# Down products of a two-unit chunk and of the last chunk put in another order, and the last layer's final norms on VectorE alone

## The reference

```python
# first layer (no convolution), hidden width 2816
gate, up = jnp.split(h @ w_ffn_in, 2, axis=-1)
y = (jax.nn.silu(gate) * up) @ w_ffn_out
# second and third layer
def conv_ffn(h, w_up, conv_w, conv_b, w_down):
    u = h @ w_up
    ...                                   # 3-tap convolution along the tokens
    a, g = jnp.split(acc, 2, axis=-1)
    return (jax.nn.silu(g) * a) @ w_down
def layer_norm(x, g, b):
    xf = x.astype(jnp.float32)
    mu = jnp.mean(xf, -1, keepdims=True)
    var = jnp.mean(jnp.square(xf - mu), -1, keepdims=True)
    return ((xf - mu) * lax.rsqrt(var + LN_EPS) * g + b).astype(x.dtype)
x_lat = layer_norm(DN_ALPHA * x_lat + m_lat[5] * f_lat, ln_g[l, 1], ln_b[l, 1])
```

## Time and profile before

| | |
|---|---|
| runs | 2518.44, 2526.46, 2524.96 us; median 2524.96 us |
| profiled execution | 2526.85 us; its span (first to last instruction) 2525.1 us |
| granted TensorE clock, mean | 0.973 of full |
| busy: PE, DVE, ACT, POOL | 2372.2, 1600.2, 974.1, 321.1 us |
| share of the span | 94%, 63%, 39%, 13% |

### The profile page before, as it was taken

One profiled execution on the slowest core, in us unless ns is written; L12 is line 12 of the kernel. 1 busy time (PEld: TensorE's weight loads), 2 busy tenths in 40 slices (PEclk: granted clock), 3 DMA queues, 4 the chain that ended last, 5 costly groups with the idle time before them and its releaser, 6 DMA issues.

```text
span 2525.1 us, 33201 instructions
## 1 busy us (share of the span) xinstructions
PE 2372.2 (94%) x13210; PEld 1915.8 (76%) x13210; DVE 1600.2 (63%) x2718; ACT 974.1 (39%) x1800; POOL 321.1 (13%) x325
## 2 busy tenths in 40 slices
PE   6988998999999899899999999999998999999996
PEld 3866567888888778566778888888887677888875
DVE  3638686565657642677778775556474987765455
ACT  4326453322212522567352232322442774423322
POOL 0210101000012200000100313223111000101223
PEclk9999999999999999999999999999998999999998
DMA  6430015744434212111412342333122103432221
GB/s 253 136 104 1 26 59 175 250 154 150 164 137 157 102 42 77 51 49 43 150 63 84 101 150 77 110 115 133 43 76 76 35 22 130 150 106 95 92 92 50
DMA packets 79162, 257.59 MB, mean 102 GB/s; under 512 B 5664, under 2 KB 10400, under 8 KB 70560
## 3 DMA queue, kind: packets, MB, share of 16 engines
q1 hardware_dynamic: 65024, 205.01, 23.6%
q0 software_dynamic: 12688, 46.14, 5.3%
q10 hardware_dynamic: 1296, 4.30, 0.4%
HBM read 246.00 MB, written 9.44 MB: 101 GB/s over the span
## 4 chain that ended last, share of the span: by engine, by line
PE 70%; DVE 14%; ACT 7%; issue 4%; DMA 2%; POOL 1%; SPq 1%; POOLq 0%; ACTq 0%; DVEq 0%
PE PS L1087 9%; PE PS L1089 9%; PE PS L1088 9%; PE PS L1158 5%; PE PS L1159 5%; PE PS L1160 5%; PE PS L948 4%; PE PS L846 3%; PE PS L843 3%; PE PS L844 3%; PE PS L961 2%; ACT HT L2469 2%; PE PS L992 2%; DVE SM L1833 1%; PE PS L891 1%
## 5 line engine op out<-in xcount | busy, mean ns | idle before, releaser
L1087 PE MATMUL PS<-HH,WH 128*128 128x512 f32 (+1 forms) x1088 | 421.3, 387 | 9.2 <-DVE TMP L2155 4.6
L1088 PE MATMUL PS<-HL,WH 128*128 128x512 f32 (+1 forms) x1088 | 417.7, 384 | 0.0
L1089 PE MATMUL PS<-HH,WL 128*128 128x512 f32 (+1 forms) x1088 | 417.7, 384 | 0.0
L2307 ACT ACTIVATE WH<-STG 128x1024 fp32r<-128x1024 f32 (+1 forms) x204 | 198.9, 1022 | 293.3 <-PE PS L1160 250.3
L2007 DVE TENSOR_TENSOR WL<-STG,WH 128x1024 fp32r<-128x1024 f32 (+1 forms) x204 | 242.4, 1230 | 48.7 <-ACT WH L2307 48.7
L1158 PE MATMUL PS<-WH,AH 128*128 128x512 f32 x616 | 247.7, 402 | 13.8 <-DVE WL L2007 5.0
L1159 PE MATMUL PS<-WL,AH 128*128 128x512 f32 x616 | 245.5, 399 | 0.0
L1160 PE MATMUL PS<-WH,AL 128*128 128x512 f32 x616 | 244.9, 398 | 0.0
L1087 PEld LDWEIGHTS PS<-HH,WH 128*128 128x128 f32 x1088 | 205.2, 189 | 52.3 <-DVE TMP L2155 5.2
L1088 PEld LDWEIGHTS PS<-HL,WH 128*128 128x128 f32 x1088 | 205.4, 189 | 40.4 <-issue 1.0
L1089 PEld LDWEIGHTS PS<-HH,WL 128*128 128x128 f32 x1088 | 205.1, 189 | 40.5
(11 more groups left out here) (224 smaller groups left out, 4276.6 us busy)
## 6 DMA issues: line engine op xcount, KB each, us to landing
STG<-in_w_up SPq DMA_DIRECT2D x66, 1024.0 KB, 6.4
ADAW<-in_w_ada SPq DMA_DIRECT2D x96, 512.0 KB, 3.8
STG<-in_w_down SPq DMA_DIRECT2D x20, 1024.0 KB, 5.4
ADAW<-in_w_ada POOLq DMA_DIRECT2D x32, 512.0 KB, 4.0
STG<-in_w_ffn_out SPq DMA_DIRECT2D x10, 1024.0 KB, 7.0
STG<-in_ev_w_in SPq DMA_DIRECT2D x8, 1024.0 KB, 5.2
STG<-in_w_in SPq DMA_DIRECT2D x6, 1024.0 KB, 6.7
spill<-X POOLq DMA_DIRECT2D x10, 512.0 KB, 4.6
```

The source lines that it names most:

```text
L1087: e.matmul(out, h_, hh, start=c == 0, stop=False)
L1088: e.matmul(out, h_, hl, start=False, stop=False)
L1089: return e.matmul(out, l_, hh, start=False, stop=c == 7)
```

## The change

Four parts.

1. `ffn_plan` (layers 0 and 2): the downs of the two-unit chunk (units 16 and 17) are held back until behind the first up of the last chunk (unit 18). `acts` gives the last chunk's AH and AL other columns than the two-unit chunk's (`own_place`), and `acts_free` looks one chunk further back.
2. `ffn` of TensorE, layer 1: in h = 0 of each chunk but the last, units 0 to n-2 are summed for the four LAT tiles first, then the last unit of each; in the last chunk, units 0 to 2 of (2, 0), (3, 0) and (4, 0) come first, as layers 0 and 2 had it.
3. `ffn` of TensorE, layer 2, last chunk: the three sums that are started ahead are now (2, 0), (2, 1) and (3, 0). Those with h = 1 use the weights of the last step.
4. Layer 2's final norms: VectorE does (x - mean) * gain over 1024 columns, and, with ScalarE's root, * rstd + bias in two halves of 512. ScalarE has only the root, GpSimd no pass. The statistics of a half are taken by themselves, and the order of VectorE's work is written out by hand. Tile 5 is stored in two halves.

The core of the diff:

```diff
@@ -101,12 +101,20 @@
 
 
 def ffn_plan(chunks):
-    plan = []
+
+    plan, held = [], []
     for g, us in enumerate(chunks):
-        plan += [("up", g, u) for u in us]
-        for h in range(2):
-            plan += [("down", g, h, c, min(4, us[-1] + 1 - c)) for c in range(us[0], us[-1] + 1, 4)]
+        ups = [("up", g, u) for u in us]
+        downs = [("down", g, h, c, min(4, us[-1] + 1 - c)) for h in range(2) for c in range(us[0], us[-1] + 1, 4)]
+        plan += ups[:1] + held + ups[1:]
+        held = downs if own_place(chunks, g + 1) else []
+        plan += [] if held else downs
     return plan
+
+
+def own_place(chunks, g):
+
+    return chunks is WIDE and g == len(WIDE) - 1
 
 
 class Kit:
@@ -459,7 +464,8 @@
         out, off = [], 0
         for _, tts in GROUPS[L]:
             T = len(tts) * P
-            out.append([self.ff[L][n][:, off:off + len(us) * T].rearrange("p (c t) -> p c t", c=len(us)) for n in ("AH", "AL")])
+            o = off + 4 * T * own_place(CHUNKS[L], CHUNKS[L].index(us))
+            out.append([self.ff[L][n][:, o:o + len(us) * T].rearrange("p (c t) -> p c t", c=len(us)) for n in ("AH", "AL")])
             off += 4 * T
         return out
 
@@ -1177,13 +1180,13 @@
             if g < len(chunks) - 1:
                 if c == 0:
                     bs = {tt: take(("down", L, g, h, tt)) for _, tts in groups for tt in tts}
-                ahead = range(n - 1) if len(groups) == 1 and h == 0 and n == len(us) else range(0)
+                ahead = range(n - 1) if h == 0 and n == len(us) else range(0)
                 for i in ahead:
                     for tt in LAT:
                         down(pi, 0, tt, bs[tt], c, [i], us)
                 for gi, (vec, tts) in enumerate(groups):
                     for tt in tts:
-                        m = down(pi, gi, tt, bs[tt], c, range(len(ahead), n), us)
+                        m = down(pi, gi, tt, bs[tt], c, range(0 if gi else len(ahead), n), us)
                         if c + n == len(us):
                             m.then_inc(*k.pe_down.up((L, g, h, tt)))
                             freed[bs[tt]] = [k.dv_yg((L, g, h, tt))]
@@ -1191,9 +1194,10 @@
                             m.then_inc(*k.pe_down.up((L, pi)))
             elif h == 1:
                 ahead = {}
-                for tt in LAT[:3] if len(groups) == 1 else ():
-                    ahead[tt, 0] = take(("down", L, g, 0, tt))
-                    down(pi - 1, 0, tt, ahead[tt, 0], 0, range(n - 1), us)
+                tails = [(LAT[0], 0), (LAT[0], 1), (LAT[1], 0)] if L == 2 else [(tt, 0) for tt in LAT[:3]]
+                for tt, hh in tails:
+                    ahead[tt, hh] = take(("down", L, g, hh, tt))
+                    down(pi - 1 + hh, 0, tt, ahead[tt, hh], 0, range(n - 1), us)
                 for gi, (vec, tts) in enumerate(groups):
                     for tt in tts:
                         for hh in range(2):
@@ -1570,7 +1574,7 @@
 
 
 def acts_free(k, L, g):
-    return k.ends(("wo", L)) if g == 0 else [k.pe_down((L, g - 1, 1, GROUPS[L][-1][1][-1]))]
+    return k.ends(("wo", L)) if g == 0 else [k.pe_down((L, g - 1 - own_place(CHUNKS[L], g), 1, GROUPS[L][-1][1][-1]))]
 
 
 def vector_program(k, e, w):
@@ -2122,8 +2115,33 @@
             ready = [x_added(k, L, g, h, tt) for h in range(2)]
             if L == 0:
                 rms(("fin", tt), tt, ready + [k.lg_in[0](("f", 0))], F["LG"][:, 0:1024])
-            elif L == 2 or tt in LAT:
+            elif tt in LAT:
                 layer_norm("f", L, tt, ready)
+
+        def last_stats(tt, h):
+
+            w.wait_ge(*x_added(k, 2, len(chunks) - 1, h, tt))
+            e.bn_stats(k.small("ln", tt, 6 * h, 6), k.x(tt)[:, h * 512:(h + 1) * 512]).then_inc(*k.dv_sum.up((("f", 2, tt), "half", h)))
+
+        def last_scaled(tt):
+
+            key, x, lg, ag = ("f", 2, tt), k.x(tt), k.ln_gain("f", 2), k.small("ln", tt, 12, 2)
+            w.wait_ge(*k.dv_sum((key, "half", 0)))
+            w.wait_ge(*k.dv_sum((key, "half", 1)))
+            e.bn_aggr(ag, k.small("ln", tt, 0, 12)).then_inc(*k.dv_sum.up((key, 1)))
+            w.wait_ge(*k.dv_sum((key, 1)))
+            variance(key, ag[:, 1:2], k.small("ln", tt, 14), 1.0, 1e-5)
+            w.wait_ge(*k.lg_in[0](("f", 2)))
+            e.scalar_tensor_tensor(out=x, in0=x, scalar=ag[:, 0:1], in1=lg[:, 0:1024], op0=ALU.subtract,
+                                   op1=ALU.mult).then_inc(*k.dv_sub.up(key))
+            root_inverse(key, k.small("ln", tt, 14), k.small("ln", tt, 15))
+            w.wait_ge(*k.dv_rstd(key))
+            w.wait_ge(*k.dv_sub(key))
+            w.wait_ge(*k.lg_in[1](("f", 2)))
+            for h in range(2):
+                s = slice(h * 512, h * 512 + 512)
+                e.scalar_tensor_tensor(out=x[:, s], in0=x[:, s], scalar=k.small("ln", tt, 15), in1=lg[:, 1024:2048][:, s], op0=ALU.mult,
+                                       op1=ALU.add).then_inc(*k.dv_ln.up((key, h)))
 
         turn_mid(L, 1)
         late = None
@@ -2172,6 +2190,27 @@
                         for _, tts in groups:
                             for tt in tts:
                                 residual(g, h, tt)
+                elif h == 1 and L == 2:
+                    t2, t3, t4, t5 = LAT
+                    for tt, hh in ((t2, 0), (t2, 1), (t3, 0)):
+                        residual(g, hh, tt)
+                    last_stats(t2, 0)
+                    last_stats(t2, 1)
+                    residual(g, 1, t3)
+                    last_scaled(t2)
+                    last_stats(t3, 0)
+                    last_stats(t3, 1)
+                    residual(g, 0, t4)
+                    residual(g, 1, t4)
+                    last_scaled(t3)
+                    last_stats(t4, 0)
+                    last_stats(t4, 1)
+                    residual(g, 0, t5)
+                    last_stats(t5, 0)
+                    last_scaled(t4)
+                    residual(g, 1, t5)
+                    last_stats(t5, 1)
+                    last_scaled(t5)
                 elif h == 1:
                     for _, tts in groups:
                         for tt in tts:
@@ -2182,8 +2221,6 @@
                             elif late is not None and (L, tt) != (0, LAT[-1]):
                                 after(late)
                             late = tt
-                    if L == 2:
-                        after(late)
             step(bg, ffn_steps(L, pi))
         step(bg, 100)
 
@@ -2667,8 +2704,10 @@
                             elif tt == LAT[-2]:
                                 for c in range(8):
                                     modulated(1, 1, c)
-                        elif L == 2 or tt in LAT:
+                        elif L == 1 and tt in LAT:
                             layer_norm("f", L, tt)
+                        elif L == 2:
+                            root(("f", 2, tt), k.small("ln", tt, 14))
                 if L == 1:
                     for c in range(8):
                         modulated(2, 0, c)
@@ -2935,14 +2966,15 @@
                 w.wait_ge(*x_added(k, L, g - 1, h, tt))
             e.tensor_tensor(xs, xs, F["YS"][:, r % n_ys * 512:(r % n_ys + 1) * 512], ALU.add).then_inc(*k.pl_x.up((L, g, h, tt)))
 
-        def after(tt):
-            if L:
-                layer_norm(L, tt)
-            if L == 2:
-                w.wait_ge(*k.ln_ready("f", 2, tt))
-                e.dma_start(k.out[(tt - 2) * P:(tt - 1) * P, :], k.x(tt)).then_inc(*k.out_st[tt - 2].up())
-
-        late = None
+        def output(tt):
+            rows, last = slice((tt - 2) * P, (tt - 1) * P), tt == LAT[-1]
+            if last:
+                w.wait_ge(*k.dv_ln((("f", 2, tt), 0)))
+                e.dma_start(k.out[rows, 0:512], k.x(tt)[:, 0:512]).then_inc(*k.out_st[4].up())
+            w.wait_ge(*k.dv_ln((("f", 2, tt), 1)))
+            s = slice(512 if last else 0, 1024)
+            e.dma_start(k.out[rows, s], k.x(tt)[:, s]).then_inc(*k.out_st[tt - 2].up())
+
         for pi, q in enumerate(plan):
             if q[0] == "up":
                 for gi, (vec, tts) in enumerate(groups if L else ()):
@@ -2963,10 +2995,10 @@
                         for tt in tts:
                             for hh in range(2):
                                 residual(g, hh, tt)
-                            if late is not None:
-                                after(late)
-                            late = tt
-                    after(late)
+                            if L == 2 and tt != LAT[0]:
+                                output(tt - 1)
+                    if L == 2:
+                        output(LAT[-1])
 
     blocks = row_blocks(1, 4)
     project(0, blocks)
```

24 lines of the change are left out of this document (1 added, 23 removed).

## The result

| | before | after |
|---|---|---|
| median of the runs | 2523.6 us (14 runs of this comparison) | 2509.43 us (14 runs) |
| lowest and highest | 2518.44, 2528.79 us | 2502.8, 2518.01 us |
| ratio after / before | | 0.995, 95% interval 0.994 to 0.996 |
| profiled execution, span | 2526.85, 2525.1 us | 2518.01, 2516.2 us |
| granted TensorE clock in it | 0.973 | 0.973 |

The change makes the kernel 0.5% faster, 12.6 us by the ratio (10 to 15). The forecast was 2517, worked out from a median of 2524.96 us before; the median came 7.6 us lower, 0.6 us under the range of 2510 to 2523 and 3.6 us under the forecast's own of 2513 to 2520.5. Taken from the same 2524.96 us the ratio gives 2512.3, inside the wide range and just under the narrow one. The profiled execution of the changed kernel is the slowest of its 14 runs, so between the two profiles only 8.8 us are gone (2526.85 - 2518.01).

The account below looks back on a forecast made before the run. TensorE was taken to bound 70% of the chain, VectorE's norms and the last store the last 23 us. -5.0 + 1.7 - 4.2 - 1.0 = -8.5 us gave 2518.3 (profile) or 2516.5 (median); said 2517, 8-in-10 range 2510 to 2523.

Parts of the forecast that it names:

- Third layer's two-unit chunk, -5.0: Holding back its downs removes 6.1 us of idle and half-clock loss, less a new wait up to 1.1 us: -5.0 us.
- behind such an idle time the stretches show the granted clock at 0.50: TensorE runs at 1.2 GHz after waits of 3.11 and 3.19 us, for 6.7 and 3.4 us.
- First layer, +1.7: Two-unit chunk's second down waits 2.15 us behind modulation sums, 0.9 more than before, plus 0.8 for clock: +1.7 us.
- Half a drop: First layer, behind the 2.15 us wait: half of one 3.4 us low-clock stretch charged, 0.8 us.
- Second layer, -4.2: Last chunk: sums done ahead cover the 3.19 us WL wait and remove the low clock behind it: -4.2 us.
- the wait forecast for the transposes: Second layer's end: TensorE waits 0.8 us before its transposes, for VectorE's last tile and ScalarE's pass.
- The rival of the other chunks' order: Follow-up's rival, second layer: other chunks' new order adds worth, undoing it costs 3 to 5 us; no chance given.
- Parts 3 and 4, -1.0: Third layer's tail: TensorE idles 5.5 us, then low clock; VectorE ends 27.0 us after LOW of (2, 0): -1.0 us.
- The store: End of the third layer: the last store holds half a tile, so takes 0.65 us less.
- the rival without a low clock (2513): New waits bring no low clock and the tail stays with VectorE: about -11.5 us, 2513; chance 0.20.
- The slower rival: Clock stays low behind the first layer's and the tail's new long waits: +5.0 us, 2530; chance 0.08.

Follow-up runs that it names:

- e7: Changed kernel with the first layer's four modulation sums done behind the two-unit chunk's second down's LOW: 2509.36 us, ratio 0.9952.
- e6: Changed kernel with the second layer's downs back in their old order: 2519.89 us, ratio 0.9995 to the kernel before.
- e10: Changed kernel with first-layer sums late, third layer's old sums ahead, second layer's new order in its last chunk only: 2506.28 us, ratio 0.9919.
- e3: Kernel before with only the new final norms and the last tile stored in halves: 2521.38 us, ratio 0.9983.
- e1: Changed kernel with the third layer's last chunk again starting (2, 0), (3, 0), (4, 0) ahead: 2506.44 us, ratio 0.9927.
- e11: Changed kernel without any edit, profiled and timed again: 2509.89 us, ratio 0.9931 to the kernel before.
- e2: Changed kernel with the third layer's last-chunk sums ahead in the order (2, 0), (3, 0), (2, 1): 2506.3 us, ratio 0.9933.

## Why the prediction was right, and where its sizes were off

**Third layer's two-unit chunk, -5.0.** The mechanism was right: the wait moved to the second down's WL, at 1.11 us (0.9 to 1.1 said), without a low clock. Between the two profiles shown the stretch is 125.9 - 121.1 = 4.8 us shorter. But the step "behind such an idle time the stretches show the granted clock at 0.50" made a rule of a single case: only one of four profiles with this gap had the drop. The mean worth is 2.7 us, 2.0 of it the idle time itself.

**First layer, +1.7.** The idle time was 2.28 us for the 2.15 said, and the sums were its cause (e7). Half a drop was charged; of five kernels with this gap one had one (e6). Not foreseen: the next block of downs takes 16.6 or 18.6 us in the five kernels with part 1 and the sums early, and 18.0 to 19.5 in those without part 1, as a low stretch at its start begins earlier or is gone. No run shows why. So over the whole stretch the term came out near -1 and not as +1.7.

**Second layer, -4.2.** The right place and mechanism. The last chunk's downs gained 5.0 us, and the wait forecast for the transposes did not come: they took 3.91 us for 3.65 without idle time. From the last up's end to the end of the block it is 41.4 to 36.6 us, -4.8. Over the longer stretch it is 6.8 us in the mean and 4.1 between the two profiles shown. The rest goes with fewer low stretches in the third layer's attention part (20.5 us of them in each of the three kernels without part 2, 15.4 in the mean of the ten with it); that part 2 is what spares them was not shown. The rival of the other chunks' order is excluded by e10.

**Parts 3 and 4, -1.0.** Here the chain of steps held nearly to the tenth: idle 5.36 us (5.5), low clock behind, (2, 0) at 14.2 us into the tail (14.4), VectorE 26.8 us from there (27.0), the tail 1.1 us shorter. e3 and e1 show the two terms apart: -5.4 and +4.3. The store is the one term that came out at half its size (0.3 for 0.65). The drop was 3.4 us long in e11 and 6.8 in the profile shown, with tails of 44.6 and 44.9, but about half of the longer one fell into the idle time: TensorE worked through 2.9 and 3.4 us of it. In e2 it worked through 5.8 us of it, and the tail gained 0.9 us where 2 had been expected with a half clock.

The Trainium skill, page "SBUF — State Buffer", section "SBUF: two separate sides", had been weighed for up to 0.4 us on a store issued beside a VectorE pass. The page ties that hold to a VectorE operation in a two-port mode, and nothing here shows the half pass to be one. The half store was issued at 2512.02, 0.3 us behind the end of its half pass (2510.98 + 0.7 = 2511.7), while the other half ran. The store at 2494.63, with no such pass beside it but statistics of the next tile, came 0.3 us behind too (2492.92 + 1.41 = 2494.33). Nothing of that hold is to be seen here.

**The total.** -8.5 agrees with the two profiles shown (-8.8) and is 4 us short of the 12.6 us by the ratio. The agreement with the profiles is in part luck. Place by place they differ by -4.8 (third layer), -0.8 (first layer), -4.1 (second layer) and -1.1 us (tail), together -10.8; the stretches for which nothing was forecast took back 2.0 (+2.6 in the second layer's other chunks, within their scatter, and -0.6 ahead of the first layer's second chunk). By the number alone the rival without a low clock (2513) lies nearer to the 2512.3 us of the ratio than the forecast does; but its condition did not hold, as a low clock followed the 5.36 us in all five profiles. Against the means over the profiles (-11.8), the sum was 2.3 us too good in the third layer, where it took a drop for certain that comes once in four; 2.9 too bad in the first layer; 2.6 too small in the second, where it left out what came beyond the last chunk; and right in the tail. The mean clock over runs agrees: 0.974 in the runs of the kernel before that were timed beside the experiments, 0.978 in the 14 of the changed one. Why the chip lowers the clock behind one gap and not behind its twin stays open; no run here controls it. The slower rival (a low clock of over 12 us in the tail) did not occur: no low stretch that met the tail's downs was longer than 6.8 us.

## What to carry to other kernels

Count what stands between the last thing to arrive and the first results that the next engine needs, not the idle time of the engine that waits. The old order of the sums brought TensorE's gap from 5.36 to 0.61 us; the tail gained 4.3 us because (2, 0) was then whole ahead of the wait and not 21 matmuls behind it, and (2, 1) 12 behind it and not 24 (e1). A gap 2 us shorter, with 12 matmuls for 21, gave only 0.9 us, all 12 at half clock (e2). When a change has parts at different places, test each apart: the norms gained 5.4 us, and the sums ahead that came with them took 4.3 of it back, which no comparison of the two whole kernels shows. A pair of kernels whose runs scatter by 0.3% is best compared stretch by stretch, over several kernels that share the stretch; a clock drop seen once is a chance, not a cost.

## What was not expected of the hardware

- A gap of 3.11 to 3.12 us at the same instruction was followed by half clock in one of four profiles; one of 3.19 to 3.20 us in the second layer in all three; one of 5.36 us in all five, for 3.4 or 6.8 us; one of 3.35 us in its one profile (e2), for 6.8 us; one of 2.28 us in one of five; one of 1.11 us in none of nine.
- The length of the gap does not decide alone. The prediction charged no drop behind a gap shorter than 1.21 us, which came true at its place but is no rule: in the second layer a gap of 0.84 to 0.86 us stands in six profiles, the one of the kernel before among them, and half clock came with it in every one. Ahead of it TensorE had done 32 matmuls of one column. TensorE there and the stretch behind, in the kernel before:

```profile
1513.88 3.63 PE L752 MATMUL PS<-CON,ACC 128*128 128x1 f32 x32
1518.35 0.47 PE L1158 MATMUL PS<-WH,AH 128*128 128x512 f32 x1 [0.84 <-DVE TMP L2155]
...
1519.10:1522.50 3.40, 3.40 (x9) 2.67 (x8) 2.62 (x11) 2.31 (x3) 0.16 (x1) 0.50 0.00 0
```

- The same kernel's span differed by 10.1 us between two executions with the same gaps, at clocks of 0.973 and 0.978.
- Four sums of 1.22 us each took 7.97 us beside GpSimd's adds (e7), 64% more than before the move, and three of those adds took 2.3 us each for 1.3; in the tail a pass over 1024 columns 2.23 us for 1.27, while the GpSimd add beside it took 1.29 us, no longer than its neighbours.
